# A fused decoder block on one core: its opening in four feature groups of 256, with four weight subtractions moved to GpSimd

## The reference, cut to what matters

```python
mod = silu(c) @ w_ada + b_ada                 # c: 1024; w_ada: 1024 x 6144
shift1, scale1, ... = split(mod, 6)
h = rmsnorm(x, g_norm1) * (1 + scale1) + shift1
z = h @ w_in                                  # w_in: 1024 x 8712
xr, gr, q, k, v, fl, mg = split(z, ...)       # xr, gr: 1280 columns each
xr = causal_dwconv(xr, w_rnn_conv)            # 4 taps
hr = rg_lru(xr, ...)                          # two 128x128 gate products per block, then a scan
y_rnn = gelu(gr) * hr
```

## Time and profile before

| | before |
|---|---|
| median of 3 runs | 962.19 us (962.09 to 962.51) |
| span of the profiled execution, first to last instruction | 960.0 us |
| TensorE busy | 949.8 us, 99% |
| VectorE busy | 633.6 us, 66% |
| ScalarE busy | 415.0 us, 43% |
| GpSimd busy | 10.3 us, 1% |
| mean granted TensorE clock | 0.998 |
| chain that ended last | TensorE 97% |

### The profile page before, as it was taken

How to read it: one execution, slowest core, us unless ns; L and a number is a source line. 1 busy time by engine, 2 the same in 40 slices (tenths; PEclk the granted TensorE clock), 3 DMA queues, 4 the chain that set the end, 5 groups by cost and what they waited for, 6 DMA issues and landing times.

```text
span 960.0 us, 12336 instructions
## 1 busy us (share of the span) xinstructions
PE 949.8 (99%) x4662; PEld 803.8 (84%) x4662; DVE 633.6 (66%) x856; ACT 415.0 (43%) x548; POOL 10.3 (1%) x33
## 2 busy tenths in 40 slices
PE   8999999999999999999999999999999999999997
PEld 8788888888988888989888898888888888888885
DVE  4889998522578787854678447776764345756845
ACT  6679777222246263454424464223222232422511
POOL 0120000000000000000000000000000000000000
PEclk9999999999999999999999999999999999999999
DMA  9753312336555536332236504656533422252101
GB/s 331 256 154 99 98 44 72 98 98 211 179 155 173 183 115 203 115 104 74 88 129 222 175 23 143 208 178 206 184 94 118 161 87 87 91 215 89 44 23 66
DMA packets 106287, 129.43 MB, mean 135 GB/s; under 512 B 5260, under 2 KB 81796, under 8 KB 106124
## 3 DMA queue, kind: packets, MB, share of 16 engines
q1 hardware_dynamic: 105864, 128.38, 40.7%
q10 hardware_dynamic: 388, 0.58, 0.2%
HBM read 126.81 MB, written 2.14 MB: 134 GB/s over the span
## 4 chain that ended last, share of the span: by engine, by line
PE 97%; DVE 1%; ACT 1%; issue 0%; POOL 0%; DVEq 0%; POOLq 0%; ACTq 0%
PE ps L1778 31%; PE ps L1780 31%; PE ps L1779 31%; PE ps L1845 1%; PE ps L2038 1%; DVE ada_acc L1117 1%; PE ps L1865 0%; PE ps L2167 0%; PE ps L1828 0%; ACT htmp L727 0%; DVE wsplit L1242 0%; PE ps L1837 0%; ACT h L730 0%; ACT wsplit L722 0%; DVE o_nat L1770 0%
## 5 line engine op out<-in xcount | busy, mean ns | idle before, releaser
L1778 PE MATMUL ps<-h,wsplit 128*128 128x512 f32 (+1 forms) x816 | 312.1, 383 | 0.0
L1780 PE MATMUL ps<-h,wsplit 128*128 128x512 f32 (+1 forms) x816 | 310.8, 381 | 0.0
L1779 PE MATMUL ps<-h,wsplit 128*128 128x512 f32 (+1 forms) x816 | 310.7, 381 | 0.0
L1094 DVE TENSOR_TENSOR wsplit<-wraw,wsplit 128x2048 fp32r<-128x2048 f32 (+2 forms) x78 | 164.7, 2112 | 93.4 <-ACT wsplit L681 61.8
L1780 PEld LDWEIGHTS ps<-h,wsplit 128*128 128x128 f32 x816 | 153.4, 188 | 29.6
L1778 PEld LDWEIGHTS ps<-h,wsplit 128*128 128x128 f32 x816 | 153.5, 188 | 28.8 <-issue 0.2
L1779 PEld LDWEIGHTS ps<-h,wsplit 128*128 128x128 f32 x816 | 153.5, 188 | 28.5
L681 ACT ACTIVATE wsplit<-wraw 128x2048 fp32r<-128x2048 f32 (+2 forms) x68 | 119.0, 1750 | 101.8 <-PE ps L1780 101.4
L1712 DVE SCALAR_TENSOR_TENSOR cv<-ps,vec,cv 128x511 f32<-128x511 f32 (+1 forms) x48 | 35.9, 748 | 53.8 <-ACT cv L1049 50.7
L1151 DVE SCALAR_TENSOR_TENSOR ada_acc<-ada_raw,small,ada_acc 128x512 f32<-128x512 f32 x84 | 63.1, 751 | 2.8
L1778 PE MATMUL ps<-wsplit,act_s 128*128 128x512 f32 x160 | 62.2, 389 | 0.0
(11 more groups left out here) (258 smaller groups left out, 1387.9 us busy)
## 6 DMA issues: line engine op xcount, KB each, us to landing
wraw<-in_w_ffn_up SPq DMA_DIRECT2D x24, 1024.0 KB, 5.1
wraw<-in_w_in SPq DMA_DIRECT2D x23, 1024.0 KB, 5.3
ada_raw<-in_w_ada SPq DMA_DIRECT2D x16, 1024.0 KB, 7.1
wraw<-in_w_ffn_down SPq DMA_DIRECT2D x10, 1024.0 KB, 4.9
ada_raw<-in_w_ada_final SPq DMA_DIRECT2D x8, 1024.0 KB, 5.1
ada_first<-in_w_ada SPq DMA_DIRECT2D x7, 1024.0 KB, 11.8
wraw<-in_w_in SPq DMA_DIRECT2D x12, 512.0 KB, 3.9
wraw<-in_w_proj_rnn SPq DMA_DIRECT2D x8, 640.0 KB, 4.3
```

What stands on the lines that cost most here:

```text
L1094: ve.tensor_tensor(wsplit[:, s, LO, 0:n], wraw[:, s, 0:n], wsplit[:, s, HI, 0:n].bitcast(F), ALU.subtract).then_inc(w_lo, 1)
L1778: te.matmul(dst, lhs(LO), rhs(HI), start=start, stop=False)
L1779: te.matmul(dst, lhs(HI), rhs(LO), start=False, stop=False)
L1780: return te.matmul(dst, lhs(HI), rhs(HI), start=False, stop=stop)
```

## The change

- The opening works in **four groups of 256 features** (two k each). `ada_first` now holds per group and k the 256 shift columns beside the 256 scale columns, so one piece of 128x512 on VectorE covers both. The loads have rows of 1 KB in place of 2 KB. Of the first group TensorE takes k 0, 1, 4, 6 directly and VectorE the other four; of the groups after it VectorE takes all eight.
- The three weight chunks come in quarters of two k. TensorE's products go group by group: chunks 0, 1, 2 with k 0 and 1, then with k 2 and 3, and so on (`first_products`), with the totals of groups 1, 2, 3 between them.
- GpSimd makes the low parts of chunk 1 and 2 in groups 1 and 2, four subtractions of 128x512 (`w_low` in its list). VectorE makes the other eight.
- x is transposed feature block by feature block; `htmp` of k = 0 is made by VectorE from PSUM, k = 1 by ScalarE from PSUM. The scaling of x is done in pieces of 256 and 768 columns.
- TensorE waits for both gelus before `rnn_gates(0)`, no longer after it, and the PSUM banks of the opening change.

```diff
+N_GROUPS = KD // 2
-        ada_first = at("ada_first", 128, [P, 6, 4, T])
+        ada_first = at("ada_first", 128, [P, 3, KD, 2, 256])
...
+        ADA_PE = (0, 1, 4, 6)
+        ADA_DVE = [[k for k in range(KD) if g or k not in ADA_PE] for g in range(N_GROUPS)]
...
+            def load_first(g, k0, k1):
+                for v in range(2):
+                    sp.dma_start(ada_first[:, g % 3, k0:k1, v], w_ada_pairs[:, k0:k1, v, 256 * g:256 * g + 256])\
+                      .then_inc(ada_landed(g, k0), 16)
...
+            for k0 in range(0, KD, 2):
+                load_first(0, k0, k0 + 2)
+            load_rows_of(wraw_r0, COL_XR, 0, wg_first_loaded)
...
+            load_rows_of(wraw[:, 1], COL_GR, 0, wg_loaded[0])
+            load_rows_of(wraw[:, 0], COL_XR + 256, 0, wg_loaded[0])
+            for g in range(1, N_GROUPS):
+                if g == 3:
+                    sp.wait_ge(ada_mm, 1)
+                load_first(g, 0, 4)
+                load_first(g, 4, KD)
+                load_rows_of(wraw_r0, COL_XR, g, wg_loaded[g])
+                load_rows_of(wraw[:, 1], COL_GR, g, wg_loaded[g] if g < 3 else w_loaded[1])
+                load_rows_of(wraw[:, 0], COL_XR + 256, g, wg_loaded[g] if g < 3 else w_loaded[0])
...
@@ gpsimd
+            def w_low(g, j):
+                raw = wraw[:, 1 if j == 1 else 0]
+                split = wsplit[:, 1 if j == 1 else 0]
+                sl = slice(512 * g, 512 * g + 512)
+                pool.wait_ge(wh_hi, 3 * g + j + 1)
+                pool.tensor_tensor(split[:, LO, sl], raw[:, sl], split[:, HI, sl].bitcast(FP32), ALU.subtract)\
+                    .then_inc(wp_lo, 1)
+            for g in range(1, 3):
+                for j in range(1, 3):
+                    w_low(g, j)
...
@@ scalar
+            first_hi(wsplit_r0, wraw_r0, 0, wg_first_loaded, 16, wh_hi)
+            first_hi(wsplit[:, 1], wraw[:, 1], 0, wg_loaded[0], 32, wh_hi)
+            ae.wait_ge(h_tmp, 1)
+            ae.activation(h[:, HI, 0], htmp[:, 0], ACT.Copy).then_inc(h_hi, 1)
+            h_high(1)
...
@@ vector
+            for b in range(2, NB):
+                xn1(b, slice(0, 256))
+            ada_first_sums(0, range(0, 3))
+            for b in range(2, NB):
+                xn1(b, slice(256, D))
+            ada_first_sums(0, range(3, len(ADA_DVE[0])))
+            store_first(0)
+            ve.wait_ge(xT_mm, 1)
+            ve.tensor_scalar(htmp[:, 0], ps[:, XT_BANK[0], :], gs1[:, 0:1], mod[:, M_SH1:M_SH1 + 1],
+                             ALU.mult, ALU.add).then_inc(h_tmp, 1)
+            w_low(0, 0)
             h_low(0)
+            w_low(0, 1)
             h_low(1)
+            ada_first_sums(1, range(0, 3))
+            w_low(0, 2)
+            ada_first_sums(1, range(3, KD))
+            w_low(1, 0)
+            store_first(1)
...
@@ tensor
+            first_products(0, 0)
+            te.wait_ge(xT_copied, 2)
+            first_products(0, 1)
+            te.wait_ge(xT_copied, 6)
+            te.wait_ge(vec_loaded, 16 * 7)
...
+            ada_first_total(1)
+            first_products(0, 2)
+            first_products(1, 0)
+            first_products(1, 1)
+            ada_first_total(2)
+            first_products(1, 2)
+            first_products(2, 0)
+            first_products(2, 1)
+            ada_first_total(3)
+            first_products(2, 2)
+            for j in range(3):
+                first_products(3, j)
+            te.wait_ge(gelu_done, 2)
             rnn_gates(0)
             te.wait_ge(w_lo, whole(C_RNN + 1, 1))
-            te.wait_ge(gelu_done, 2)
+            te.wait_ge(conv_tap, 6)
```

More of the change, by code:

```diff
@@ L714, in _ @@
-            for b in range(NB - 1):
-                xn1(b)
-            for b in range(NB):
-                xT_copy(b)
-            def hi_half(split, raw, half, loaded, count=16):
-                ae.wait_ge(loaded, count)
-                sl = slice(1024 * half, 1024 * half + 1024)
-                ae.activation(split[:, HI, sl], raw[:, sl], ACT.Copy).then_inc(w_hi if half else wh_hi, 1)
+                ae.activation(x_nat[:, b, part], x_nat[:, b, part], ACT.Copy, scale=rs1[:, b:b + 1])\
+                  .then_inc(xn1_done, 1)
@@ new lines, in _, with first_hi, xT_copy @@
+            for part in (slice(0, 256), slice(256, D)):
+                for b in range(2):
+                    xn1(b, part)
+            def first_hi(split, raw, g, loaded, count, done):
+                ae.wait_ge(loaded, count)
+                sl = slice(512 * g, 512 * g + 512)
+                ae.activation(split[:, HI, sl], raw[:, sl], ACT.Copy).then_inc(done, 1)
+            def xT_copy(n):
+                k = XT_ORDER[n]
+                ae.wait_ge(xT_mm, 3 + (2, 3, 4, 5, 6, 7).index(k))
+                ae.activation(xT_out[:, k], ps[:, XT_BANK[k], :], ACT.Copy).then_inc(xT_copied, 1)
@@ new lines, in _ @@
+            ae.activation(h[:, HI, 0], htmp[:, 0], ACT.Copy).then_inc(h_hi, 1)
+            h_high(1)
+            xT_copy(0)
+            xT_copy(1)
+            first_hi(wsplit[:, 0], wraw[:, 0], 0, wg_loaded[0], 32, wh_hi)
+            for n in range(2, 6):
+                xT_copy(n)
+            first_hi(wsplit_r0, wraw_r0, 1, wg_loaded[1], 48, wh_hi)
+            ae.wait_ge(vec_mm, 2)
+            ae.activation(vec[:, V_ROWS_A:V_END], ps[:, 6, V_ROWS_A:V_END], ACT.Copy).then_inc(vec_ok, 1)
@@ L1794, in project, with first_products @@
                 return ins
-            def project2(split, x_, bank, k0, k1, ready):
-                for k in range(k0, k1):
-                    ready(k)
+            def first_products(g, j):
+                split = (wsplit_r0, wsplit[:, 1], wsplit[:, 0])[j]
+                if g in (1, 2) and j:
+                    te.wait_ge(wp_lo, 2 * g + j - 2)
+                elif g < 3:
+                    te.wait_ge(wh_lo, j + 1 if g == 0 else g + 3)
+                else:
+                    te.wait_ge(w_lo, RING + j + 1)
+                for k in range(2 * g, 2 * g + 2):
+                    te.wait_ge(h_lo, k + 1)
                     for t in range(2):
-                        ins = mm3(ps[:, bank + t, :],
-                                  lambda part: split[:, part, k * 256 + P * t:k * 256 + P * t + P], features(x_, k),
+                        if (g, j, k, t) == (0, 0, 0, 1):
+                            te.wait_ge(h_tmp, 2)
+                        ins = mm3(ps[:, FIRST_BANKS[j] + t, :],
+                                  lambda part: split[:, part, k * 256 + P * t:k * 256 + P * t + P], features(h, k),
                                   k == 0, k == KD - 1)
@@ L1868, in _, with x_transposes @@
-            te.wait_ge(cact_done, 1)
-            ada_piece(0, 0, 0, begin=True)
+            keep_clock(14, 7)
+            def x_transposes(k):
+                if k < 2:
+                    te.wait_ge(xn1_done, 2)
+                    te.wait_ge(newton_step, 6)
+                else:
+                    te.wait_ge(xn1_done, 4)
+                    te.wait_ge(newton_step, 8)
+                if k == 6:
+                    te.wait_ge(vec_ok, 1)
+                if k == 7:
+                    te.wait_ge(ada_out, 2)
+                for b in range(NB):
+                    ins = te.transpose(ps[:, XT_BANK[k], P * b:P * b + P], x_nat[:, b, P * k:P * k + P], ident[:, :])
+                ins.then_inc(xT_mm, 1)
@@ L1882, in _ @@
[L1882 to L1891 removed]
+            ada_piece(4)
@@ L1894, in rnn_gates @@
+            keep_clock(2, 7)
+            ada_piece(6)
+            ada_first_total(0)
+            for k in range(2, KD):
+                x_transposes(k)
             def rnn_gates(i):
```

330 lines of the change are left out of this document (119 added, 211 removed).

## The result

| | before | after |
|---|---|---|
| median of 4 runs each | 962.14 us (961.88 to 962.51) | **966.89 us** (965.98 to 967.83) |
| profiled execution: time, span, mean granted clock | 960.0 (span), 0.998 | 966.34, 964.5, 0.993 |
| first product of the opening | 25.61 | 20.41 |
| first product of GR+256 | 65.63 | 70.03 |

The ratio is 1.0050, 95% interval 1.0036 to 1.0063: slower, and 4.4 us above the forecast of 962.5 (range 959.3 to 964.7). The anchor point did its work: GR+256 came 4.40 us later, the span grew by 4.5.

The account below looks back on a forecast made before the run. TensorE, busy 949.8 of 960.0 us, bounds the kernel; only its opening can be won. GR+256 from 65.63 to 63.5, plus 2.4 for GpSimd's hold of VectorE, gives 65.9: 962.19 + 0.3 = 962.5 us, range 959.3 to 964.7.

Parts of the forecast that it names:

- The anchor point: TensorE's first product of GR+256, at 65.63 us before: the kernel is shorter or longer by as much as this moves.
- Step 1 and 2: Opening loads and first product: 1 KB rows at 352 GB/s, three quarters landed at 19.3, first product from 25.61 to 21.4.
- Step 3: VectorE's list until GR+256: 0.5 us longer but started earlier; eight sums spaced 0.78 take 6.0 us.
- Step 4 and 6: TensorE without memory dispute: waits 1.8, 0.6, 0.85, GR+256 at 63.5; afterwards VectorE 2.6 late within slack, softplus hidden.
- Step 5, the hold: GpSimd's four subtractions, 1.0 us each, hold VectorE as long; TensorE waits 2.4 us more, GR+256 at 65.9.
- Rival B: GpSimd's subtractions long and held, from 1.5 us each; new TensorE waits could also cost its clock: 964.2 to 966, chance 0.20.

Follow-up runs that it names:

- with pieces: Changed kernel with 20 or 25 front fills, TensorE taking piece k = 0 of groups 1 to 3, one VectorE wait per load: 962.33 to 962.47 us.
- The first round's pair: Changed kernel, 966.89 us, against the same kernel with VectorE making GpSimd's four low parts itself, 964.36 us.
- the first experiment: Changed kernel plus 10 and 6 keep_clock matmuls without a use ahead of totals 1 and 3: 967.55 us, ratio 1.0066.
- front 25: Changed kernel with 25 instead of 14 keep_clock matmuls ahead of the first w_ada piece, none between the pieces: 964.93 us, ratio 1.0031.
- front 20: Changed kernel with 20 instead of 14 keep_clock matmuls ahead of the first w_ada piece, those between pieces kept: 964.86 us, ratio 1.0030.
- the changed kernel again: The changed kernel with no further edit, run once more in the last round: 967.92 us, ratio 1.0052.
- the delayed one: Changed kernel with 12 keep_clock matmuls between the low part of h and the first product: 967.85 us, ratio 1.0065.

## Why the prediction was wrong

**Step 1 and 2, loads and first product:** better than predicted in the profile after, 20.41 against 21.4. That was luck: of the 15 profiles of the changed kernel's variants and of itself again, two more lie below 21.4 (20.95 and 20.98), the others at 21.68 to 26.64. The rate was right (348 GB/s for rows of 1 KB, 352 taken); the lag of the chunk's quarters was smaller.

**Step 3, the spacing of the sums:** 0.85 instead of 0.78. Five take 4.16, which is four spacings and one sum of 0.75; counted in the same way the five in 3.97 before the change are spaced 0.80. The new piece waits for its load and for the sum before it; with one wait per load five take 3.96. Over seven spacings that is 0.3 to 0.4 us in a group, an estimate.

**Step 4 and 6, the stops:** total 1 at 28.95 (29.1 predicted), two stops before GR+256 that make 4.08 us of the 12 gate products (4.2 predicted), no gap from 70 to 170 us, softplus hidden at 54.7 to 63.1. These came as said. The waits for the totals came in part: 2.40 us at total 1 (1.8 predicted), none at total 2 (0.8), which TensorE itself reached late, and 1.55 at total 3 (1.3).

**Step 5, the hold:** right in kind and in both directions, with 1.28 to 1.33 us for an operation in the profile after where 1.0 was taken, and 4.1 us taken from VectorE where 3.1 was. But it is a small part of what made the kernel slower. With 20 or 25 fills in front the pairs with and without GpSimd differ by 0.4 us or less in their medians, and not in its disfavour; in the profiles the way from first product to GR+256 is longer with GpSimd by 0.4 us, and by 0.7 with pieces. (The first round's pair, 966.9 and 964.4, compares executions with different losses of clock.) The prediction summed it against a case in which VectorE has neither the hold nor its own 2.4 us for the four low parts, and such a kernel was not run.

The Trainium skill (SBUF — State Buffer, "Who interferes with whom") has the lock on both sides; the traces now show both. The Trainium skill's GPSIMD Engine Reference ("Elementwise — side-by-side cycle accounting") gave an estimate of 1.12 us; the measured 1.28 to 1.33 decides, and the two back to back took 3.00.

**The step that failed** is the price of TensorE's new waits, which left out the clock. The prediction read "1.00 granted in all windows now, longest idle 0.70" and then put waits of 1.8, 0.8 and 1.3 us into step 4 and 5 at the price of the waits alone. The loss of clock behind them stood only in Rival B, as a rider to a slow GpSimd, at "10 such products add 2.3". It needed no slow GpSimd. In the profile after it hit 12 products behind total 1 (5.26 us instead of 3.00, and 0.6 on the total itself) and about seven of the 12 behind total 3 (the 12 in 4.32 instead of 3.00). Some of that VectorE would have made TensorE wait for anyway: from total 1 to total 2 the profile after takes 12.39 us, the kernel with 20 fills in front, which kept the clock there, 10.75. So 1.6 of the 4.1 us between 65.9 and 70.03 come from the first loss and about 1.3 from the second (from total 3 to GR+256 17.6 us, and 16.3 with the fills at the totals). Some 0.8 are the sums' spacing and the longer GpSimd operation in two groups; 0.4 are not assigned. These shares come from comparing profiles of different kernels. The edit that bears on them most directly is the first experiment's: with both waits filled, no clock is lost from 25 us on, and first product to GR+256 takes 46.12 us instead of 49.62, from a later start.

**What no step had:** the shorter fill in front. It turns the early start, the gain the change is about, into one that some executions don't get at all. The two kernels that change only these fills (25 and none between, or 20) are 2 us lower in the median (964.86, 964.93), on another chip than the 14 fills ran on in any experiment. Taking the low parts from GpSimd gave 2.5 (964.36), so the front is not the largest effect of a single edit either. Part of the 2 us is the loss it moved: a late first product shortens the wait at total 1.

**The pace.** The deeper reason why 5.2 us of an earlier first product bring nothing is that the product waits for VectorE at every total. Between first product and GR+256 the kernel before takes 40.0 us, the changed one with the clock at 1.00 from 25 us on 44.2 to 46.2, with TensorE's pieces 43.6 to 44.3. TensorE's products are the same. They start up to 5 us earlier, and 4 to 6 us more go into waits, totals and the fills there. Four groups mean three loops of total, store, sums where two groups had one, and a loop through VectorE's list takes 10.4 to 10.8 us without GpSimd where TensorE needs 9.5. With pieces, 10.3 from total to total, the kernel is level with the one before and no better.

## What to carry to other kernels

When an edit makes TensorE wait where it did not, price the products behind the wait at half clock as a case of its own, and look at the fills that the edit shortens as closely as at the work it moves. Measure the kernels that are to be compared on the same chip. An earlier start is worth only what the slowest loop behind it lets through: add up one round of that loop, on the engine that closes it, before counting the start as a gain. Where a profile shows one execution and the runs spread by more than the kernel before does, sort the runs by their clock before comparing medians.

## What the runs showed of the hardware

- The same kernel had two openings in two profiled executions: first product at 20.41 or at 26.64, by whether a load landed before or after TensorE ran out of fills. The fills' own speed moved too: 14 of them took 3.32 to 4.46 us in seven profiles.
- The same wait can cost the clock or not: behind idle of 1.53 to 1.57 at total 3 the clock halved in three profiles (after, front 25, front 20) and stayed in two (the changed kernel again, and the delayed one). Behind 0.70 to 1.05 at a total or a low part it never fell, behind 2.40 it did. At the front it fell behind 1.31, 1.39 and 1.79 and not at once behind 0.51 to 0.68.
- The clock also fell with TensorE busy all the time, behind some 6 us of one-column products, transposes and few fills (24 transposes in 4.34 us instead of 2.82). Of nine profiles in which TensorE does not stop between 10 and 20 us this was in eight, and not in that of the result. Of four more that stop for 0.06 to 0.68 us and lose nothing at once, two have it and two do not, so it is not a fixed cost of this stretch. The Trainium skill (TensorE: Matmul & The Clock Gate, "Part 4: PE-mode transpose") says that transposes do not count as busy in the same way; no run here tells them from the one-column products.
- A held VectorE operation can be tiny: one of ten columns took 1.26 us instead of 0.16.
